# Front of the pooling layer: loads in the order of use, small vectors in its middle, map halves and row turns one step later

## What is computed

```python
def pool_layer(x, buf, pos0, g_norm, w_in, w_map, scale, w_out):
    uz = rmsnorm(x, g_norm) @ w_in                 # w_in: 1024 x 4096
    u, z = uz[..., :D_A], uz[..., D_A:]            # D_A = 2048
    u_ext = jnp.concatenate([buf, u], axis=1)
    mix = multiscale_pool(u_ext, pos0)             # windows 2, 4, 8, 16, a group each
    mix = jnp.einsum('btgi,gio->btgo', mix.reshape(b, t, 4, 512), w_map)
    mix = mix.reshape(b, t, D_A) * scale
    y = (mix * jax.nn.silu(z)) @ w_out
    return x + y, u_ext[:, -POOL_BUF:]
```

## Time and profile before

| | us |
|---|---|
| median of 3 runs | 3113.91 (3110.49 to 3114.06) |
| the profiled execution | 3111.94 |
| its span in the trace | 3109.8 |
| TensorE busy in the span | 2981.7 (96%) |
| ScalarE, VectorE busy | 1269.1, 1583.3 |

### The profile page before, as it was taken

The page is one execution under the profiler, slowest core; times in us unless marked ns, Lnnn a source line. Parts: engine busy times, 40 slices in busy tenths (PEclk is TensorE's granted clock), DMA queues, the critical chain, the costliest instruction groups (busy, mean ns, idle before and its releaser), DMA issues. The chain is left out here.

```text
span 3109.8 us, 45931 instructions
## 1 busy us (share of the span) xinstructions
PE 2981.7 (96%) x17416; PEld 2486.6 (80%) x17416; DVE 1583.3 (51%) x2678; ACT 1269.1 (41%) x2236; POOL 128.1 (4%) x171
## 2 busy tenths in 40 slices
PE   7999999999989999899999999979999999988898
PEld 5888888878977888788888888869999999855786
DVE  2355555464442111343443433348888888644654
ACT  3444343342221000343333432247777777633332
POOL 0000000000000000000000000010000000021220
PEclk9999999999999999999999999989999999999999
DMA  7433433432525222355654654662444444399452
GB/s 225 135 134 129 139 119 115 149 127 86 191 79 173 98 91 88 118 203 169 198 178 164 199 167 168 189 158 52 104 109 108 105 102 107 111 417 408 157 175 101
DMA packets 272279, 470.06 MB, mean 151 GB/s; under 512 B 23818, under 2 KB 124666, under 8 KB 266074
## 3 DMA queue, kind: packets, MB, share of 16 engines
q1 hardware_dynamic: 270049, 467.47, 46.5%
q0 software_dynamic: 2048, 0.14, 0.0%
HBM read 356.93 MB, written 111.34 MB: 151 GB/s over the span
## 5 line engine op out<-in xcount | busy, mean ns | idle before, releaser
L1716 ACT ACTIVATE attn_scores<-attn_scores,attn_lowest 128x1024 f32<-128x1024 f32 (+15 forms) x256 | 306.8, 1203 | 12.2 <-DVE attn_lowest L1769 12.1
L1769 DVE CUSTOM_DVE_ANT_0 attn_scores<-attn_s,region_early 128x1024 f32<-128x1024 f32 (+7 forms) x256 | 216.6, 856 | 107.9 <-POOL region_early L1622 38.4
L207 PE MATMUL pool_acc<-pool_odd_x_hi,pool_wl 128*128 128x512 f32 (+1 forms) x640 | 226.1, 353 | 0.0
L205 PE MATMUL pool_acc<-pool_odd_x_hi,pool_wh 128*128 128x512 f32 (+1 forms) x640 | 224.7, 351 | 0.0
L206 PE MATMUL pool_acc<-pool_odd_x_lo,pool_wh 128*128 128x512 f32 (+1 forms) x640 | 223.6, 349 | 0.0
L205 PE MATMUL outa_acc<-outa_w_hi,outa_g_hi 128*128 128x512 f32 x512 | 202.1, 395 | 18.2 <-DVE outa_w_lo L997 14.1
L205 PE MATMUL pool_acc<-even_x,pool_wh 128*128 128x512 f32 x512 | 203.3, 397 | 0.0
L206 PE MATMUL pool_acc<-even_x,pool_wh 128*128 128x512 f32 x512 | 202.5, 395 | 0.0
L207 PE MATMUL pool_acc<-even_x,pool_wl 128*128 128x512 f32 x512 | 202.5, 395 | 0.0
L206 PE MATMUL outa_acc<-outa_w_lo,outa_g_hi 128*128 128x512 f32 x512 | 201.0, 393 | 0.0
L207 PE MATMUL outa_acc<-outa_w_hi,outa_g_lo 128*128 128x512 f32 x512 | 200.8, 392 | 0.0
(11 more groups left out here) (271 smaller groups left out, 6662.7 us busy)
## 6 DMA issues: line engine op xcount, KB each, us to landing
pool_wz<-in_w_in_a SPq DMA_DIRECT2D x18, 2048.0 KB, 8.5
pool_wu<-w_mix SPq DMA_DIRECT2D x16, 2048.0 KB, 8.0
region_early<-in_w_kv SPq DMA_DIRECT2D x16, 2048.0 KB, 9.5
region_early<-in_w_in_b SPq DMA_DIRECT2D x16, 2048.0 KB, 8.9
hold_kq<-in_cache_k SPq DMA_DIRECT2D x64, 512.0 KB, 10.1
region_early<-in_cache_v SPq DMA_DIRECT2D x64, 512.0 KB, 10.0
region_early<-gatedT SPq DMA_DIRECT2D x16, 1024.0 KB, 5.5
gatedT<-pool_gates SPq DMA_DIRECT2D x48, 256.0 KB, 2.2
```

The costliest lines, as they stand in the source:

```text
L205: pe.matmul(out, ah, bh, start=first, stop=False)
L207: return pe.matmul(out, al, bh, start=False, stop=last)
L1716: act.activation(part, part, ACT.Exp, scale=-1.0, bias=low[s][:, x:x + 1], accum_out=sums[s][:, i:i + 1]).then_inc(expd, 1)
L1769: dve.tensor_tensor_reduce(sc[s][:, c, a0:a0 + n], s_ps[idx % 2][:, 0:n], bias[h % 2][:, b0:b0 + n], -SCALE, low[s][:, x - 2:x - 1] if x > ...
```

## The change

Three edits, all in the order of instructions; none is added or removed.

```diff
-NORM_FIRST = {0: 0, 1: 8, 2: 13, 3: 16, 4: 21}
+NORM_FIRST = {0: 0, 1: 8, 2: 12, 3: 16, 4: 20}
+MAP_AT = {1: 0, 2: 1, 3: 2, 6: 3}
...
-            return [(b, i - s) for b, s in NORM_FIRST.items() if 0 <= i - s <= 3]
+            return [(b, i - s) for b, s in NORM_FIRST.items() if 0 <= i - s <= 4]
...
             norm.load(sp, 0)
+            self.load_map(sp, 1)
             sp.dma_start(state, ...).then_inc(state_in, 16)
-            self.load_raw(sp, 1)
-            self.load_map(sp, 1)
-            norm.load(sp, 1)
-            norm.load(sp, 2)
...
+            def further_loads(x):
+                if x == 0:
+                    self.load_raw(sp, 1)
+                elif x == 1:
+                    norm.load(sp, 1)
+                    norm.load(sp, 2)
...
             for x in range(NI):
                 g, k = divmod(x, KC)
                 sp.wait_ge(w_copied, x + 1)
                 sp.dma_start(D["w_mix"][...], mix[x % GC][:, :]).then_inc(w_out[x % GC], 16)
+                further_loads(x)
                 for b, step in first_norm_steps(x):
-                    if step == 2 and b + 3 < first_block[1]:
+                    if step == 3 and b + 3 < first_block[1]:
                         norm.load(sp, b + 3)
...
-                elif step == 3 and b:
+                elif step == 4 and b:
                     norm.high(act, b)          # and norm.low on VectorE alike
...
-                if k < GC:
-                    map_high(g + 1, k)
+                if k in MAP_AT:
+                    map_high(g + 1, MAP_AT[k]) # and map_low on VectorE alike
...
                 for b, step in first_norm_steps(x):
-                    if step == 2:
+                    if step == (3 if b else 2):
                         norm.turn(pe, b)
...                                             # main loop
                 for b, step in norm_steps(p, g, i):
-                    if step == 2:
+                    if step == 3:
                         norm.turn(pe, b)
```

More of the change, by code:

```diff
@@ L393, in _ @@
             norm.load(sp, 0)
+            self.load_map(sp, 1)
             sp.dma_start(state, D["state_pool"][0].rearrange("b t c -> (b t) c")).then_inc(state_in, 16)
-            self.load_raw(sp, 1)
-            self.load_map(sp, 1)
-            norm.load(sp, 1)
-            norm.load(sp, 2)
[L399 to L404, removed]
+            def further_loads(x):
[4 more added lines that the diff above has]
+                    norm.load(sp, 2)
+                elif x == KC + 1:
+                    for t, n in zip(self.vec, ("lambda_q1", "lambda_k1", "lambda_q2", "lambda_k2")):
+                        sp.dma_start(t, D[n][0].partition_broadcast(P)).then_inc(lam_in, 16)
+                elif x == KC + 2:
+                    sp.dma_start(D["pool_sample"][0, :, 0:HIST - TS, :], D["state_pool"][0, :, TS:HIST, :]).then_inc(old_out, 16)
+                elif x in range(2 * KC, 2 * KC + len(columns)):
+                    tile, vector = columns[x - 2 * KC]
+                    sp.dma_start(tile[:, :], vector.rearrange("(k p) -> p k", p=P),
+                                 allow_slow_non_contiguous=True).then_inc(columns_in, 16)
             for x in range(NI):
@@ L733, in _ @@
                 turned_low(x + 2)
-                if k < GC:
-                    map_low(g + 1, k)
+                if k in MAP_AT:
+                    map_low(g + 1, MAP_AT[k])
                 for b, step in first_norm_steps(x):
```

## The result

| | before | after |
|---|---|---|
| median (4 runs each) | 3112.93 (3110.49 to 3114.06) | 3093.82 (3092.90 to 3094.45) |
| ratio, 95% interval | | 0.9939, 0.9924 to 0.9955 |
| span of the profiled execution | 3109.8 | 3091.7 |

A forecast was written before the change was run, and what follows sets the result against it. TensorE, busy 2981.7 of 3109.8 us, bounds the kernel, so only its idle time can be won. 11.9 + 1.2 + 4.65 − 2.1 = 15.65 us saved gives a forecast of 3097 us, range 3093 to 3100.5 (0.80).

The forecast's parts named there:

- The long wait: Pooling layer's front, row transposes (L177) after iteration 2: earlier map cuts the wait from 12.95 to 1.0, saving 11.9 us.
- The clock: Iteration 3 in the front: TensorE's clock no longer falls behind the shorter idle time, saving 1.2 us.
- L811: Pooled sample rows, iterations 14 and 22: earlier block starts add waits of 0.65 and 1.45, costing 2.1 us.
- The main loop: Pooling layer's main loop: row turns one step later remove three waits of the row transposes, saving 1.5 us.
- Edits costed at nothing: Raw weights, row blocks, small vectors and state copy loaded later, in the loop: no cost, as they land in time.
- The sum: Whole kernel: savings of 11.9, 1.2 and 4.65 less a cost of 2.1 give 15.65 us.
- the front's short waits: Front of the pooling layer: row turns one step later remove two other waits of the row transposes, saving 3.15 us.

The follow-up runs named there:

- the repeat: The changed kernel run once more, unaltered, to show the spread between executions: median 3094.4 us, ratio 0.9935.
- e8: Changed kernel with blocks 2 and 4 started at 13 and 21, third doubling at k = 4, square-root table loaded first: 3090.3 us, ratio 0.9929.
- e7: Changed kernel with blocks 2 and 4 started at 13 and 21 as before: 3092.4 us, ratio 0.9937.
- e4: Changed kernel with only group 1's map moved ahead of the state, all other loads before the loop again: 3103.9 us, ratio 0.9967.
- e9: Kernel before, old order of state, raw weights and map and old steps, but small loads and row blocks in the loop: 3111.7 us, ratio 0.9989.
- e10: Changed kernel with only group 1's raw weights before the loop again, behind the state: 3094.7 us, ratio 0.9936.
- e1: Kernel before with the new order of loads alone; map quarters, block starts and row turns as before: 3102.6 us, ratio 0.9965.
- e6: Changed kernel with TensorE's row turns of the main loop back at step 2: 3101.0 us, ratio 0.9966.
- e11: Changed kernel with lambda vectors, column vectors and the old state's copy before the loop again: 3091.3 us, ratio 0.9924.
- e5: Changed kernel with group 1's map issued behind the state instead of ahead of it: 3101.4 us, ratio 0.9960.

## Why the prediction was right, and where it was off

**The long wait: right.** The map landed at 18.3, the quarter was bound by ScalarE, and L177 kept 1.04 us; forecast 1.0. The start, 22.19, is 0.4 before the forecast of 22.6 by the luck of the clock; the repeat has 22.52. By the 1.38 us of drain behind a table load that the Trainium skill gives ("ScalarE: Activation LUTs", section "What ACT_TABLE_LOAD costs") the wait would have been 2.4. The root began at 20.43, 1.29 after the load at 19.14 began, and in e8 the whole wait shrank by 0.84 when the load left the path. No drain is seen.

**The clock: right, a little low.** From L177's start to the transposes at 53.71 the kernel before took 19.19 us, the changed one 39.77 − 22.19 = 17.58: 1.6 for 1.2. I had counted only the matmuls; the transposes of L177 and the way to the next instruction ran at half clock too, 35.56 − 34.52 = 1.04 us instead of 22.83 − 22.19 = 0.64. The reason that I gave for no fall, an idle time of 1.74 us at a clock of 1.00, held.

**L811: right as a mechanism and nearly in size.** Waits of 0.95 and 1.35 for 0.65 and 1.45, sum 2.3 for 2.1. In the trace the copy for the doublings of iteration 20 began 103.37 − 101.25 = 2.1 us behind the split (before 0.6), for 2.2 forecast, and e7 shows that the earlier start is the cause.

**The main loop: mis-sized.** The term "those of the main loop 1.5" measured 2.5. The listed idle times are 0.75, 0.41 and 0.33, the gains at the same places 1.2, 0.75 and 0.55. I had taken the listed idle time for the cost of a wait. It begins at the modelled end of the last matmul, which overlaps the next when nothing waits (0.40 us long, at a distance of 0.23); each wait costs some 0.3 us more, by the starts. The same holds for the front's short waits: in e7, which takes both away and adds none, the stretch from the first transposes of group 1 to the first matmul of the main loop is 3.6 us shorter than before, for 3.15 listed.

**"Edits costed at nothing": wrong for the loads moved into the loop.** Where they stand now they cost nothing, as I wrote, and the raw weights came in time. But I drew from it that their move was worth nothing, so that the map's place alone carried 11.9 us. e4 and e9 show that the move (in e9 without the raw weights, which e10 finds to be worth 0.1) is worth 10.0 us once the wait is gone and 0.2 as long as it is there. The forecast holds all the same, because the change that it forecast includes the move; how much of it the sum owed to the move was not seen. I had asked what the stores cost where they are now, and not what hid their lateness before: in the old order SP issued the first three only at 33.65, and the wait for the map covered that.

**The sum.** 15.65 forecast, 17.3 and 17.6 measured at the end of the pooling layer: 0.4 more from the clock and 1.0 from the main loop. The front's short waits and L811 together gave 1.1 for 3.15 − 2.1 = 1.05, as the two errors there cancel. The rest, 0.4 and in the repeat 0.1, comes from where the clock rose. The time, 3093.8, lies in the range, near its lower end.

## What to carry to other kernels

When a long wait goes, look for what it has been hiding: list everything that was late inside it, above all the DMA queue's own instructions, since a store that is issued 20 us late shows in no list of waits as long as nobody asks for its buffer. Put loads that are needed late behind the first stores, small ones above all, and one that blocks a serial engine ahead of everything it doesn't need. Read the gain of an order change at the first instruction behind the changed part, and count a short wait of TensorE from start to start.

## What the runs showed of the hardware

- The clock fell with shorter idle times than I thought safe. In e1, with 3.5 us of it, it was at 0.80 between 22 and 24 us, while TensorE still stood, and at 0.50 after. In e6 a wait of 2.17 us was enough, and the fall came after TensorE had begun again: 0.57 between 680 and 684 us. With 1.04 us (after), 1.74 (before) and 1.90 (e1, at 61 and at 96 us) it stayed at 1.00.
- SP can sit long in the issue of one DMA: 8.51 us (e4) and 12.60 us (e11) for the 0.5 KB of one column vector, where 0.4 to 0.9 are usual. The kernel before has such issues too, 7.45 us for the map and 7.73 for the same column vector. Each time several loads had been issued and had not yet landed; what limits it was not tried.
- Two executions of one program agree within 0.3 us at the end of the pooling layer (889 us) and differ by 3.1 in the span. The first loads can vary more, as the 2.4 us of e5 show. What makes the later layers differ is open.
